# Second feed forward of a two-block transformer kernel: chunks three to ten with the weights on the stationary side and 256-column products

## What is computed

```python
def second_block(x, norm_mix, w_in, w_up_a, w_up_b, w_out, norm_ffn, w_gate, w_up, w_down, norm_final):
    ...
    x = x + merged @ w_out[layer]
    h = rmsnorm(x, norm_ffn[layer])
    x = x + (jax.nn.silu(h @ w_gate[layer]) * (h @ w_up[layer])) @ w_down[layer]
    return rmsnorm(x, norm_final)
```

## Time and profile before

| | |
|---|---|
| median of 3 runs | 738.89 us |
| the profiled execution | 738.71 us |
| its span, first to last instruction | 736.9 us |
| PE busy | 721.7 us (98%) |
| DVE busy | 506.2 us (69%) |
| ACT busy | 398.4 us (54%) |
| granted PE clock, mean | 0.997 |

### The profile page before, as it was taken

One profiled execution on the slowest core, in us unless ns is written; L12 is line 12 of the kernel. 1 busy time (PEld: TensorE's weight loads), 2 busy tenths in 40 slices (PEclk: granted clock), 3 DMA queues, 4 the chain that ended last, 5 costly groups with the idle time before them and its releaser, 6 DMA issues.

```text
span 736.9 us, 9728 instructions
## 1 busy us (share of the span) xinstructions
PE 721.7 (98%) x3816; PEld 576.6 (78%) x3816; DVE 506.2 (69%) x900; ACT 398.4 (54%) x653; POOL 24.6 (3%) x44
## 2 busy tenths in 40 slices
PE   6999999999999999999999999999999999999996
PEld 5568885568888888888878777778888888888885
DVE  4477999899668555565988799865857545544544
ACT  3367336886666545456545667666456344434432
POOL 1020011000100000000010000000000000000000
PEclk9999999999999999999999999999999999999998
DMA  9994939954464655545528543345365555655511
GB/s 325 367 392 161 349 123 349 376 174 156 161 226 172 229 179 213 175 155 193 158 96 302 184 133 116 115 162 180 115 229 196 198 178 183 208 180 171 172 58 57
DMA packets 80845, 144.90 MB, mean 197 GB/s; under 512 B 4048, under 2 KB 35792, under 8 KB 80800
## 3 DMA queue, kind: packets, MB, share of 16 engines
q1 hardware_dynamic: 78992, 138.98, 55.2%
q0 software_dynamic: 1520, 5.03, 1.9%
q10 hardware_dynamic: 288, 0.27, 0.1%
HBM read 143.22 MB, written 1.05 MB: 196 GB/s over the span
## 4 chain that ended last, share of the span: by engine, by line
PE 89%; DVE 4%; DMA 2%; issue 2%; SPq 1%; ACT 1%; POOL 0%; POOLq 0%; DVEq 0%
PE bank L413 23%; PE bank L415 22%; PE bank L414 22%; PE bank L730 5%; PE bank L395 5%; PE bank L728 3%; DMA W<-in_w_in 2%; PE bank L432 2%; DVE WL L1475 1%; SPq L293 1%; PE bank L572 1%; PE bank L594 1%; PE bank L846 1%; PE bank L868 1%; PE bank L727 1%
## 5 line engine op out<-in xcount | busy, mean ns | idle before, releaser
L1475 DVE TENSOR_TENSOR WL<-W,WH 128x1024 fp32r<-128x1024 f32 (+1 forms) x214 | 248.6, 1208 | 47.5 <-ACT WH L998 47.2
L998 ACT ACTIVATE WH<-W 128x1024 fp32r<-128x1024 f32 (+1 forms) x214 | 210.5, 1042 | 70.3 <-DMA W<-in_w_mlp 40.9
L413 PE MATMUL bank<-WH,AHL 128*128 128x512 f32 (+1 forms) x512 | 203.1, 397 | 1.4 <-DVE AHL L1484 1.0
L415 PE MATMUL bank<-WH,AHL 128*128 128x512 f32 (+1 forms) x512 | 198.0, 387 | 0.0
L414 PE MATMUL bank<-WL,AHL 128*128 128x512 f32 (+1 forms) x512 | 197.7, 386 | 0.0
L413 PEld LDWEIGHTS bank<-WH,AHL 128*128 128x128 f32 x512 | 96.2, 188 | 27.7 <-issue 6.1
L415 PEld LDWEIGHTS bank<-WH,AHL 128*128 128x128 f32 x512 | 96.2, 188 | 20.1
L414 PEld LDWEIGHTS bank<-WL,AHL 128*128 128x128 f32 x512 | 96.4, 188 | 17.8
L413 PE MATMUL bank<-WH,HH 128*128 128x512 f32 (+1 forms) x218 | 84.9, 390 | 0.0
L415 PE MATMUL bank<-WH,HL 128*128 128x512 f32 (+1 forms) x218 | 84.5, 388 | 0.0
L414 PE MATMUL bank<-WL,HH 128*128 128x512 f32 (+1 forms) x218 | 84.4, 387 | 0.0
(11 more groups left out here) (260 smaller groups left out, 775.0 us busy)
## 6 DMA issues: line engine op xcount, KB each, us to landing
W<-in_w_mlp SPq DMA_DIRECT2D x32, 1024.0 KB, 5.5
W<-in_w_in SPq DMA_DIRECT2D x28, 1024.0 KB, 6.0
W<-in_w_ada SPq DMA_DIRECT2D x12, 1024.0 KB, 8.0
WX<-in_w_ada SPq DMA_DIRECT2D x12, 1024.0 KB, 10.1
W<-in_w_gate SPq DMA_DIRECT2D x22, 512.0 KB, 4.2
W<-in_w_up SPq DMA_DIRECT2D x22, 512.0 KB, 5.4
W<-in_w_down SPq DMA_DIRECT2D x11, 1024.0 KB, 4.9
W<-in_w_out SPq DMA_DIRECT2D x8, 1024.0 KB, 5.4
```

The source lines that it names most:

```text
L413: e.matmul(po, hs, wh[:, k, c0:c0 + cw], start=first and k == 0, stop=False)
L415: ins = e.matmul(po, ls, wh[:, k, c0:c0 + cw], start=False, stop=last and k == unit.nk - 1)
L998: e.activation(m.WH[unit.slot][:, c], m.W32[unit.slot][:, c], ACT.Copy).then_inc(S["w_hi"], 1)
L1475: e.tensor_tensor(m.WL[unit.slot][:, c], m.W32[unit.slot][:, c], m.WH[unit.slot][:, c].bitcast(F32), ALU.subtract).then_inc(S["w_lo"], 1)
```

## The change

Chunks 2 to 9 of the second feed forward get a new product `up2_features(c)`. It puts 128x128 blocks of `WH` and `WL` on the stationary side and streams the activations of all 256 tokens: for each of the two units, each of four feature blocks j (two of gate, two of up, banks 4 to 7) and each of four k, three matmuls of 256 columns. Gate and up come out with the features on the partitions, so these chunks have no `hid_turn2`. ACT's Silu (`silu_features`) and DVE's multiplication (`gated_features`) work on blocks of 128 features x 256 tokens; high and low parts are made from `hid` in SBUF (`high_features`, `low_features`) instead of from a bank. ACT and DVE now split both gate/up units first, then do Silu or the multiplication of both halves, then the down unit. The first gate/up slot of a chunk is free after half of the product, the second at its end. The semaphore `m1_up` of the first feed forward is renamed `up_block` and counts on; `HID2` gives the order of the halves.

```diff
-GU_ORDER = [(0, 0), (1, 0), (0, 1), (1, 1)] + [(c, tb) for c in range(2, 11) for tb in range(2)]
-GU_AT = {ct: 2 * i + 2 for i, ct in enumerate(GU_ORDER)}
+GU_ORDER = [(0, 0), (1, 0), (0, 1), (1, 1)]
+GU_AT = {ct: 2 * i + 2 for i, ct in enumerate(GU_ORDER)} | {(10, tb): 18 + 2 * tb for tb in range(2)}
+HID2 = {ct: i + 1 for i, ct in enumerate(GU_ORDER + [(c, p) for c in range(2, 11) for p in range(2)])}
...
             for i in range(2):
-                add(("gu", c), "w_gate_2", 4 * i, 4, [("w_gate_2", 256 * c, 256), ("w_up_2", 256 * c, 256)],
-                    True, ("gu_mm", GU_AT[c, 1] - 1 + i))
+                if 1 < c < 10:
+                    free = ("up_block", 20 + 4 * c) if i else ("gu_mm", 7 + c)
+                else:
+                    free = ("gu_mm", GU_AT[c, 1] - 1 + i)
+                add(("gu", c), "w_gate_2", 4 * i, 4, [("w_gate_2", 256 * c, 256), ("w_up_2", 256 * c, 256)], True, free)
...
+    def up2_features(c):
+
+        for i, unit in enumerate(by["gu", c]):
+            wh = m.WH[unit.slot][:, :].rearrange("p (k n) -> p k n", k=4)
+            wl = m.WL[unit.slot][:, :].rearrange("p (k n) -> p k n", k=4)
+            for j in range(4):
+                js = slice(128 * j, 128 * j + 128)
+                po = bank[4 + j][:, 0:256]
+                if i == 0:
+                    take(4 + j)
+                for k in range(4):
+                    sem_x, value = n_ready(2, 1)(4 * i + k)
+                    w.wait_ge(S[sem_x], value)
+                    w.wait_ge(unit.lo[0], unit.lo[1] + k // 2 + 1)
+                    hs, ls = m.AH[:, 4 * i + k, :], m.AL[:, 4 * i + k, :]
+                    e.matmul(po, wh[:, k, js], hs, start=i == 0 and k == 0, stop=False)
+                    e.matmul(po, wl[:, k, js], hs, start=False, stop=False)
+                    ins = e.matmul(po, wh[:, k, js], ls, start=False, stop=i == 1 and k == 3)
+                if i:
+                    ins.then_inc(S["up_block"], 1)
+                    frees(4 + j, ("hid2" if j > 1 else "silu_g", HID2[c, j % 2]))
+            if i == 0:
+                ins.then_inc(S["gu_mm"], 1)
...
-    for c in range(1, 10):
-        if c > 1:
-            up2(c, 0)
-            up2(c, 1)
+    for tb in range(2):
+        down2(0, tb, True, False)
+    for tb in range(2):
+        hid_turn2(1, tb)
+    for c in range(2, 10):
+        up2_features(c)
         for tb in range(2):
-            down2(c - 1, tb, c == 1, False)
-        for tb in range(2):
-            hid_turn2(c, tb)
+            down2(c - 1, tb, False, False)
...
+    def silu_features(c, p):
+        w.wait_ge(S["up_block"], 4 * (c + 4) + p + 1)
+        w.wait_ge(S["hid2"], HID2[c - 1, p])
+        e.activation(m.rel[p][:, 0:256], bank[4 + p][:, 0:256], ACT.Silu).then_inc(S["silu_g"], 1)
+
+    def high_features(c, p):
+        w.wait_ge(S["hid2"], HID2[c, p])
+        w.wait_ge(S["dn_mm"], DN_AT[c - 2, 1])
+        copy(m.HH[c % 2][:, p, :], m.hid[c % 2][:, 0, 256 * p:256 * p + 256], "hid_hi")
...
     for c in range(2, 10):
+        hi(2)
+        silu_features(c, 0)
+        silu_features(c, 1)
         hi()
-        silu_gate(c, 0)
-        hi()
-        silu_gate(c, 1)
-        hi()
-        for tb in range(2):
-            hid_hi2(c, tb)
+        high_features(c, 0)
+        high_features(c, 1)
...
+    def gated_features(c, p):
+        w.wait_ge(S["silu_g"], HID2[c, p])
+        w.wait_ge(S["up_block"], 4 * (c + 4) + p + 3)
+        if c < 4:
+            w.wait_ge(S["hid_turned"], 6 + 2 * (c - 2))
+        else:
+            w.wait_ge(S["hid_lo"], 16 + 2 * (c - 2) + p + 1)
+        tt(m.hid[c % 2][:, 0, 256 * p:256 * p + 256], bank[6 + p][:, 0:256], m.rel[p][:, 0:256], ALU.mult, "hid2")
+
+    def low_features(c, p):
+        w.wait_ge(S["hid_hi"], 16 + 2 * c + p + 1)
+        tt(m.HL[c % 2][:, p, :], m.hid[c % 2][:, 0, 256 * p:256 * p + 256], m.HH[c % 2][:, p, :].bitcast(F32), ALU.subtract, "hid_lo")
...
     for c in range(2, 10):
+        lo(2)
+        gated_features(c, 0)
+        gated_features(c, 1)
         lo()
-        gated(c, 0)
-        lo()
-        gated(c, 1)
-        lo()
-        for tb in range(2):
-            hid_lo2(c, tb)
+        low_features(c, 0)
+        low_features(c, 1)
```

More of the change, by code:

```diff
@@ L146 @@
 out_mm o1_hi o1_lo res1 nscale_dve nscale_act n_turned n_dve n_act kn
-m1_mm m1_up m2_mm mlp_sum mlp_act hid_turned hid_hi hid_lo btw
+m1_mm up_block m2_mm mlp_sum mlp_act hid_turned hid_hi hid_lo btw
 qi_mm s_mm p2_mm g_mm p2_out
@@ L234, in weight_units @@
         elif c < 8:
-            for i, free in enumerate((("m1_mm", 7 + c), ("m1_up", 4 * c - 4))):
+            for i, free in enumerate((("m1_mm", 7 + c), ("up_block", 4 * c - 4))):
                 add(("m1", c), "w_mlp1", 4 * i, 4, [("w_mlp1", 512 * c, 512)], True, free)
@@ L731, in up_wide @@
                 if i:
-                    ins.then_inc(S["m1_up"], 1)
+                    ins.then_inc(S["up_block"], 1)
                     frees(4 + j, ("mlp_sum", 4 * c + j - 7))
@@ L933, in up2 @@
         product(by["gu", c], m.AH, m.AL, tb, bk, "gu_mm", n_ready(2, tb), 512, between)
-        frees(bk, ("hid2", GU_AT[c, tb] // 2))
+        frees(bk, ("hid2", HID2[c, tb]))
+    def up2_features(c):
[16 more added lines that the diff above has]
+                if i:
+                    ins.then_inc(S["up_block"], 1)
+                    frees(4 + j, ("hid2" if j > 1 else "silu_g", HID2[c, j % 2]))
+            if i == 0:
+                ins.then_inc(S["gu_mm"], 1)
     def hid_turn2(c, tb):
-        hid_turn(c, 2, tb, ("hid2", GU_AT[c, tb] // 2, 16 + 2 * c + tb + 1))
+        hid_turn(c, 2, tb, ("hid2", HID2[c, tb], 16 + 2 * c + tb + 1))
     def down2_last():
@@ L948, in down2 @@
             part(unit, m.HH[c % 2], m.HL[c % 2], 0, tb, 2 * n + tb, first, last, "dn_mm",
-                 lambda k: ("hid_lo", 16 + 2 * c + tb + 1), 512 * n, 512)
+                 lambda k: ("hid_lo", 16 + 2 * c + (k if 1 < c < 10 else tb) + 1), 512 * n, 512)
     up2(0, 0)
@@ L1405, in silu_gate @@
         if c:
-            w.wait_ge(S["hid2"], GU_AT[c - 1, tb] // 2)
+            w.wait_ge(S["hid2"], HID2[c - 1, tb])
         e.activation(m.rel[tb][:, 0:256], bank[bk][:, 0:256], ACT.Silu).then_inc(S["silu_g"], 1)
@@ L1411, in hid_hi2 @@
             w.wait_ge(S["dn_mm"], DN_AT[c - 2, tb])
-        split_hi(m.HH[c % 2], 0, 2, tb, "hid_turned", 4 + 2 * c + tb + 1, "hid_hi")
+        split_hi(m.HH[c % 2], 0, 2, tb, "hid_turned", (9 if c > 1 else 5 + 2 * c) + tb, "hid_hi")
+    def silu_features(c, p):
[6 more added lines that the diff above has]
+        copy(m.HH[c % 2][:, p, :], m.hid[c % 2][:, 0, 256 * p:256 * p + 256], "hid_hi")
     silu_gate(0, 0)
@@ L1844, in vector_program, with hid_lo @@
     lo()
-    def hid_lo(c, nj, tb, i):
-        split_lo(m.HH[c % 2], m.HL[c % 2], 0, nj, tb, "hid_turned", i if nj == 4 else i - 12, i, "hid_hi", "hid_lo")
+    def hid_lo(c, nj, tb, i, at=None):
+        split_lo(m.HH[c % 2], m.HL[c % 2], 0, nj, tb, "hid_turned", at or i, i, "hid_hi", "hid_lo")
     def sum_wide(c, j):
-        w.wait_ge(S["m1_up"], 4 * (c - 2) + j + 1)
+        w.wait_ge(S["up_block"], 4 * (c - 2) + j + 1)
         if c < 4:
@@ L1922, in vector_program @@
     between(0, 2)
-    w.wait_ge(S["m1_up"], 24)
+    w.wait_ge(S["up_block"], 24)
     norm_features(2, 0, m.mix, None)
@@ L2117, in gated @@
         bk = 4 + tb if bk is None else bk
-        w.wait_ge(S["silu_g"], GU_AT[c, tb] // 2)
+        w.wait_ge(S["silu_g"], HID2[c, tb])
         if c > 1:
-            w.wait_ge(S["hid_turned"], 4 + 2 * (c - 2) + tb + 1)
+            w.wait_ge(S["hid_lo"], 16 + 2 * (c - 2) + 2)
         tt(m.hid[c % 2][:, tb, 0:256], bank[bk][:, 256:512], m.rel[tb][:, 0:256], ALU.mult, "hid2")
     def hid_lo2(c, tb):
-        hid_lo(c, 2, tb, 16 + 2 * c + tb + 1)
+        hid_lo(c, 2, tb, 16 + 2 * c + tb + 1, (9 if c > 1 else 5 + 2 * c) + tb)
+    def gated_features(c, p):
[9 more added lines that the diff above has]
+        tt(m.HL[c % 2][:, p, :], m.hid[c % 2][:, 0, 256 * p:256 * p + 256], m.HH[c % 2][:, p, :].bitcast(F32), ALU.subtract, "hid_lo")
     norm_features(5, 1, m.ffn, None)
```

## The result

The changed kernel takes 740.13 us (median of 20 runs, 739.95 to 741.67) against 738.84 us (median of 20, 738.65 to 739.0): ratio 1.0019, 95% interval 1.0013 to 1.0025. The medians differ by 1.29 us or 0.17%, the ratio by 0.19%. The forecast was 740.3 us, 1.4 us above the kernel before. The interval reaches past it and excludes a ratio of one: the change is a little slower, not free.

The account below looks back on a forecast made before the run. PE was taken as the bound: per chunk 11.51 us of products plus 5.46 of down matmuls make 16.97 against 16.804, times eight +1.4 us, so 740.3 us was predicted. The range was 739.5 to 743.0 us.

Parts of the forecast that it names:

- The bound: From 573.64 us on, time is the sum of PE's instruction spacings; PE is busy 98% of the span.
- The transposes: hid_turn2 removed in chunks 2 to 9: 0.48 us per chunk, 0.36 own and 0.12 wider spacings; gain 3.9 us.
- The narrow products: Gate and up of chunks 2 to 9: 96 256-column matmuls, spaced 0.120, take 11.51 us per chunk instead of 11.01.
- the 94 matmuls in ten microseconds: Stretch from 120 us, each matmul with its load: 0.106 us per pair, so supply doesn't set the 0.120 spacing.
- The seam: 24 down matmuls after narrow ones: 5.46 us, 0.02 above today's 5.44; bounds 0.00 and 0.14, nearer row taken.
- The far bound: Upper bound of the down product's extra: 0.14 us, if all 24 matmuls are spaced 0.2325 instead of 0.2266.
- The sum: PE per chunk: 11.51 + 5.46 = 16.97 us against 16.804, +0.17, times eight +1.4 us.
- Columns alone: Rival for the new products: cost goes by columns, spacing 0.1133, chunk 16.34 us, total 735.2 us; chance 0.08.
- The price of the mixed block: Rival: new matmuls cost 0.1263 as in first feed forward's alternating pairs; total 745.1 us; chance 0.11, whole or part.
- Late units or banks: Rival: PE waits 1 us in each chunk for a weight unit or bank, total 748.3 us; chance 0.05.
- the forecast case: New products spaced 0.1195 to 0.1205, seam 0.00 to 0.14: 739.7 to 741.7 us, chance 0.76.
- the bound of 0.2%: Total time: about 0.2% (1.48 us) is what measurement can tell from no change; +1.4 us lies just beneath.

Follow-up runs that it names:

- the narrow product in its old place: Kernel before, gate and up products of chunks 2 to 9 as 256-column matmuls, activations still stationary, transposes kept: 743.78 us against 738.71, ratio 1.0068.
- the grouped runs: Kernel before, first feed forward's alternating wide and narrow matmuls issued four and four: 738.50 us against 738.78; sixteen and sixteen per unit: 739.46 against 738.78.
- an experiment, in the first feed forward: Kernel before, first feed forward's products as sixteen wide, then sixteen narrow matmuls per unit: 739.46 us against 738.78, ratio 1.0008.

## Why the prediction was right

**The bound.** PE's spacings were taken as the only thing that counts from 573 us on. The runs on the second feed forward bore it out: 3.9 us for the transposes, 5.1 us for the narrow form, and an unchanged time with another order on ACT and DVE.

**The transposes.** 0.48 us per group, 3.9 in all: measured alone 3.9 us, period 16.32.

**The narrow products.** 11.51 us per chunk: 11.51. The nine spacings of the earlier trace rows were enough because they have the very form of the new ones. The value was right, but its reading as "256 columns cost 0.1066 and each matmul 0.0134 more" is no more than a line through two widths, and the runs with fewer columns don't lie on it. One argument beside it was weaker than it looked: the 94 matmuls in ten microseconds were to show that PE can be supplied fast enough, but only 24 of them have a stationary operand of 128 x 128. With such a new one for each matmul no product here has a mean spacing below 0.111, so the room under the 0.120 was 0.008 us and not the 0.014 of that row. The forecast didn't suffer, since it took the 0.120 from the very form.

**The seam.** 5.46 forecast, 5.47 measured, from its nearer bound. The far bound, every down matmul at 0.2325, didn't come: the spacings after a narrow run are 0.228 to 0.236 for five matmuls, then 0.2266.

**The sum.** 16.97 per chunk forecast, 16.98 measured, so eight chunks give 1.41 us; the span shows 1.2 and the medians 1.29. Two things lie between. The first new product follows transposes that are still there, and narrow matmuls pay less for that than wide ones. The changed kernel's timeline at the first block:

```profile
573.39 0.60 PE L399 MATMUL bank<-ident,hid 128*128 128x128 f32 x4
573.75 0.36 PE L955 MATMUL bank<-AHL,WH 128*128 128x256 f32 x1
573.95 0.28 PE L956 MATMUL bank<-AHL,WL 128*128 128x256 f32 x1
```

From 573.75 to 573.95 are 0.20 us, 0.08 above the usual, where the earlier trace rows have 0.32, 0.09 above. With the spacings behind it this comes to some 0.06 us less than in a wide product. And these transposes start 0.09 us earlier than before (573.39 against 573.48 in the timeline), from a stretch that the change doesn't touch; it is a difference between the two executions, not part of the change. 1.41 - 0.06 - 0.09 = 1.26, the shift of PE's last matmul.

**The rivals.** Columns alone, 735.2 us: refuted by the change itself and by the narrow product in its old place. The Trainium skill's gap of N/2.4 + 2.5 ns ("TensorE: Matmul & The Clock Gate", section "Back-to-back issue gap", where it is the gap of isolated matmuls) would have given 109 ns at 256 columns. The trace has 120, and no width tried had a mean below 111. The price of the mixed block, 745.1: refuted by the spacing of 0.120, and the grouped runs show what the mixed block paid for: the run-in after each change to the wide form. Late units or banks, 748.3: none in the changed kernel. The same mechanism did appear in an experiment, in the first feed forward, where the cover had been only 1.1 us before.

**The chances.** Most was put on the forecast case, and it came. That it lay 0.1 us from the bound of 0.2% was said beforehand. The ratio of 1.0019 came out on the near side, but its interval lies across the bound, so the side is luck.

## What to carry to other kernels

On a PE that is never idle, price a matmul by the distance of two starts of exactly its form, found anywhere in the trace, and multiply; doubling the number of matmuls at half the width cost 0.66 us per chunk here (16.98 against the 16.32 without transposes), and that ate the 0.48 us of the transposes it saved. Turning the operands round to get rid of transposes can pay when most of the moving side keeps its full width: with high and low activations side by side the same idea gave 1.9 us where the changed kernel lost 1.3. When a product is regrouped, ask when each of its banks ends, and what else stands in the queue of the engine that reads them.

## What the runs showed of the hardware

- Products with a new 128x128 fp32r weight for each matmul are spaced 0.1115 to 0.1117 us at 200, 224 and 240 columns, 0.1150 at 248, 0.120 at 256 and 0.2266 at 512.
- After a change from 256 to 512 columns the spacings of the wide form need five matmuls to come back to 0.2266 and lose some 0.03 us in all (24 matmuls in 5.47 us); after 248 columns they don't (5.44 us). After four transposes the loss is 0.12 us.
- Which operand is stationary, weights or activations, makes no difference to the spacing (0.120 both ways at 256 columns, 0.1115 and 0.1118 at 200).
